# Adding the masked scores of two directions on VectorE before one product with the values

## The chip, the cores and the metric

The kernel runs on one core of a Trainium2 chip. Its engines are TensorE (PE in the profile; its weight loads are PEld), VectorE (DVE), ScalarE (ACT), GpSimd (POOL) and SyncE (SP), which here only issues transfers. The metric is the device time of one execution in microseconds; the median of three runs is given.

## The reference

Two layers of a token-mixing backbone over 512 latent tokens and 256 context tokens. The change lies in the gated linear attention of the token mixer, which runs forward (f) and backward (b) over chunks of 64 tokens and adds the two results:

```
g_mid  = g[:, :, GLA_CHUNK // 2 - 1][:, :, None]
scores = jnp.einsum('bnihd,bnjhd->bnhij', q * jnp.exp(g - g_mid), k * jnp.exp(g_mid - g))
scores = jnp.where(mask, scores, 0.0)
o_intra = jnp.einsum('bnhij,bnjhv->bnihv', scores, v)
o_inter = jnp.einsum('bnihd,nbhdv->bnihv', q * jnp.exp(g), s_start)
...
o = o_f + flip(o_b)
o = o * lax.rsqrt(jnp.mean(o * o, axis=-1, keepdims=True) + RMS_EPS)
```

There are 4 heads with keys of 64 and values of 128 elements. `v` is the same in both directions, so `scores_f @ v + scores_b @ v` equals `(scores_f + scores_b) @ v`. The mask keeps s <= t forward and s >= t backward within a chunk.

## The kernel before

Activations lie feature-major, [128 partitions, tiles, tokens]. Each weight matrix streams in from memory in chunks (`stream`), and is split for precision: ACT rounds a chunk to `w_hi` (L1202), POOL computes the rest `w_lo` = `raw` - `w_hi` (L840), and PE multiplies three times per tile (`split_matmul`, L903). Nearly all of PE's work is these products.

The order of all work is one list, `ORDER`, built by hand in `build_order`; every engine walks it and does its own part of each entry. The attention output of a layer is done tile by tile, a tile being 128 tokens: six tiles in layer 0 (context and latent), four in layer 1. After the first two `gate` entries and the position transform (`dft`), the loop over tiles appends for tile number a:

```
order.append(("score", L, tt))
if a == 0: order.append(("halves", L))
if a + 1 < len(tiles): ... ("gate", L, tiles[a + 1], g)   # g = 0 and 1
if a: order.append(("msq", L, tiles[a - 1]))
order.append(("o", L, tt))
if a == 0: order.append(("fold", L))
```

What the engines do for these entries:

- `gate` of a tile and direction: PE sums the decays over tokens (L1044), ACT takes three exponentials of it into `E` (L1375 to L1377), DVE multiplies them with q, k and q (L1767, L1768, L1769), and says so by `qk_ready`.
- `score`: PE multiplies decayed k and q of both directions and four heads into the PSUM tile `N` (L1057, 16 instructions in the trace). DVE copies them under the mask from `N` to `Pm` (L1777, four instructions), a tile in SBUF that was set to zero once per layer (L1764).
- `o`: PE multiplies values (`vtok`, the stationary side) with `Pm` (L1069: 4 heads by 2 directions, each two instructions in the trace, so 16 a tile, in two groups of 8), and the chunk states `S` with `E` (L1075, 32 in the trace), all summed in PSUM tile `A`. ACT squares the result into `osq` (L1384).
- `msq`: PE takes means of the squares (L1083), ACT Ln and Exp (L1395, L1396), DVE scales by it and by the gate `r` (L1786, L1791 four times), ACT rounds (`h_hi`, L1398), DVE takes the rest (`h_lo`, L1795).
- `halves` and `fold`, once per layer: the halves of the position transform are copied (L1745) and folded (L1754, L1758) on DVE, rounded on ACT (L1364), and POOL takes the rest (L868).

After `o` of the second and third tile ACT also rounds two weight chunks (`high`, L1202), which POOL follows with L840. After the last `msq` comes `wout`, whose products (L903) wait for the last `h_lo`. `Pm` and `E` have two buffers, by the tile's turn `b`.

Of the kernel before, what the change touches and what calls it, by code (L numbers as in the profile page):

```python
# [14 lines left out]
P = 128  # L15
# [4 lines left out]
HEADS, DK, DV, RANK, CHUNK = 4, 64, 128, 16, 64  # L20
# [418 lines left out]
def bass_hybrid_block(nc: bass.Bass, stream, pairs, modw, xT, pos_row, pos_col, cols, wdec, masks, mats, wide, x_keep, out):  # L439
    with ExitStack() as ctx:  # L440
        def sb(name, shape, dt=F32, stack=None):
            return (stack or ctx).enter_context(nc.sbuf_tensor(name, shape, dt))

        def sem(name):
            return ctx.enter_context(nc.semaphore(name))
# [73 lines left out]
        with mix:  # L519
            kT = sb("kT", [P, 2, TOK], stack=mix)  # L520
            qT = sb("qT", [P, 2, TOK], stack=mix)
            ktok = sb("ktok", [P, TT_ALL, KW], stack=mix)
            vtok = sb("vtok", [P, TT_ALL, VW], stack=mix)
            ls = sb("ls", [P, TT_ALL, 2 * KW], stack=mix)
            S = sb("S", [P, 2, 12, 2, DV], stack=mix)
            r_s = sb("r_s", [P, 4, TOK], stack=mix)
            early, late = ExitStack(), ExitStack()
            with early:
                lrT = sb("lrT", [33, TOK], stack=early)
                eu = sb("eu", [P, 2, KW], stack=early)  # L530
                vst = sb("vst", [P, 2, TOK], stack=early)
                zs = sb("zs", [P, 2, 2 * KW], stack=early)
                cgz = sb("cgz", [P, 2, TOK], stack=early)
                bg = sb("bg", [P, 2, TOK], stack=early)
            uF = vst
            fy = ktok[:, :, :].rearrange("p (c a) b -> p c (a b)", c=2)
            cv = zs[:, :, :].rearrange("p a b -> p (a b)")[:, 0:TOK]
            with late:
                E = sb("E", [P, 2, 2, 3, 2, P], stack=late)

                Pm = sb("Pm", [P, 2, 2, 2, 2, P], stack=late)
                osq = sb("osq", [P, 4 * P], stack=late)
                rb = sb("rb", [P, 2, 4, P], stack=late)

# [29 lines left out]
            sem("ssq_ready"), sem("rstd_ready"), sem("xnew_ready"), sem("sq_ready"), sem("sq_used"))  # L574
        haff_ready, hhi_ready = sem("haff_ready"), sem("hhi_ready")
        yn_ready = sem("yn_ready")
        hlo_ready_p, hlo_ready_v = sem("hlo_ready_p"), sem("hlo_ready_v")
        pair_in, sums_ready, f_hi, f_lo, f_used = (
            [sem(f"pair_in{j}") for j in range(2)], sem("sums_ready"), sem("f_hi"), sem("f_lo"), sem("f_used"))
# [13 lines left out]
        def nth(L, tt):  # L593

            return 6 * L + tiles_of(L).index(tt)
# [5 lines left out]
        def read_out(eng, e):  # L601

            for u, before in PLAN.before[e]:
                eng.wait_ge(free[u], before + 1)
# [57 lines left out]
        def o_at(b, h):  # L662
            pr, hp = divmod(h, 2)
            return A[b][:, hp * 512 + pr * P:hp * 512 + (pr + 1) * P]
# [226 lines left out]
        def _(pe):  # L891
# [23 lines left out]
            for e in ORDER:  # L915
                kind, L = e[0], e[1]
                n0 = PLAN.n0[e]
                if kind == "modk":
                    g, k = e[2:]
# [5 lines left out]
                    for j in range(4):  # L925
                        mm = pe.matmul(dst[32 * j:32 * j + 32, 0:512], csil[:, k, :], piece_at(p)[:, 512 * j:512 * j + 512],  # L926
                                       start=(k == 0), stop=(k == KT - 1))
# [15 lines left out]
                elif kind == "head":  # L943
# [13 lines left out]
                    m = project(dst, n, [parts(("nrm",) + pre)[s]], H, ready=lambda k: h_wait(pe, *pre, s, k))  # L957
# [7 lines left out]
                elif kind == "z":  # L965
                    tt = e[2]
# [5 lines left out]
                              start=True, stop=True).then_inc(full["z"], 1)  # L972
                elif kind == "turn":
# [4 lines left out]
                    for tt in range(TT_ALL):  # L978
                        m = pe.transpose(G[tt // 4][:, (tt % 4) * P:(tt % 4 + 1) * P], src[:, tt * P:(tt + 1) * P], ident[:, :])
                    m.then_inc(full["turn"], 1)  # L980
                elif kind == "suffix":
                    g, tt = STEPS[e[2]]
                    unit_free(e)
                    if PLAN.full[e] == 1:
# [3 lines left out]
                              start=True, stop=True)  # L988
                    for pr in range(2):
                        m = pe.matmul(N[:, 768 + 2 * pr:770 + 2 * pr], ls[:, tt, g * KW + pr * P:g * KW + (pr + 1) * P],  # L990
                                      mat[:, 768:770], start=True, stop=True)
                    m.then_inc(full["suffix"], 1)
                elif kind == "dstate":
                    g, tt = STEPS[e[2]]
# [4 lines left out]
                    for c in range(2):  # L999
                        for pr in range(2):  # L1000
                            for hp in range(2):
                                h, row = 2 * pr + hp, slice(c * 64, c * 64 + 64)
                                m = pe.matmul(G[c][hp * 64:hp * 64 + 64, pr * DV:(pr + 1) * DV],  # L1003
                                              eu[row, g, h * DK:(h + 1) * DK], vtok[row, tt, h * DV:(h + 1) * DV],
                                              start=True, stop=True)
                    m.then_inc(full["dstate"], 1)
                elif kind == "four":
                    tt = e[2]
# [3 lines left out]
                    for ch in range(2):  # L1012
                        m = pe.matmul(unit_of(e)[:, ch * 256:(ch + 1) * 256], uF[:, ch, tt * P:(tt + 1) * P], chan[:, :],
                                      start=True, stop=True)
                    m.then_inc(full["four"], 1)
                elif kind == "dft":
# [10 lines left out]
                    for ch in range(2):  # L1027
                        for a, tt in enumerate(tts):
                            for part in range(2):
# [6 lines left out]
                                for p, (l, r) in enumerate(((lhs[0], w_hi), (lhs[0], w_lo), (lhs[1], w_hi))):  # L1036
                                    m = pe.matmul(dst, l, r[:, s, o:o + w], start=(first and p == 0), stop=(last and p == 2))  # L1037
                    m.then_inc(chunk_used, 1)
                elif kind == "gate":
                    tt, g = e[2], e[3]  # L1040
# [6 lines left out]
                elif kind == "score":  # L1047
                    tt = e[2]
                    b = turn(L, tt)
# [9 lines left out]
                elif kind == "o":  # L1059
# [2 lines left out]
                    unit_free(e)  # L1062
                    read_out(pe, ("score", L, tt))
                    read_out(pe, ("dstate", L, 11))
                    for pr in range(2):
                        for g in range(2):
                            for hp in range(2):
                                h = 2 * pr + hp
                                pe.matmul(o_at(b, h), vtok[:, tt, h * DV:(h + 1) * DV], Pm[:, b, hp, g, pr, :],  # L1069
                                          start=(g == 0), stop=False)  # L1070
                        for g in range(2):
                            for c in range(2):
                                for hp in range(2):
                                    row = slice(hp * 64, hp * 64 + 64)
                                    m = pe.matmul(o_at(b, 2 * pr + hp)[:, c * 64:c * 64 + 64], S[row, g, 2 * tt + c, pr, :],  # L1075
                                                  E[row, b, g, 2, pr, c * 64:c * 64 + 64], start=False,
                                                  stop=(g == 1 and c == 1))
# [443 lines left out]
        def _(dve):  # L1521
            steps = [0]

            def link(ins):

                steps[0] += 1
                ins.then_inc(dve_step, 1)
                dve.wait_ge(dve_step, steps[0])
# [124 lines left out]
            for e in ORDER:  # L1653
# [106 lines left out]
                elif kind == "gate":  # L1760
                    tt, g = e[2], e[3]
                    b = turn(L, tt)
                    if tiles_of(L).index(tt) == 0 and g == 0:
                        link(dve.memset(Pm[:, :, :, :, :, :], 0.0))  # L1764
                    read_out(dve, e)
                    q_, k_ = qT[:, :, tt * P:(tt + 1) * P], kT[:, :, tt * P:(tt + 1) * P]
                    dve.tensor_tensor(E[:, b, g, 0, :, :], E[:, b, g, 0, :, :], q_, ALU.mult)  # L1767
# [2 lines left out]
                elif kind == "score":  # L1770
# [3 lines left out]
                        dve.wait_ge(full["o"], nth(L, e[2]) - 1)  # L1774
                    for hp in range(2):
                        for g in range(2):
                            m = dve.copy_predicated(Pm[:, b, hp, g, :, :],  # L1777
                                                    mask[:, g:g + 1, :].to_broadcast([P, 2, P]),
                                                    N[:, hp * 512 + g * 256:hp * 512 + (g + 1) * 256].rearrange("p (r t) -> p r t", r=2))
                        m.then_inc(free[f"N{hp}"], 1)  # L1780
                elif kind == "msq":
                    tt = e[2]
                    b, q = turn(L, tt), nth(L, tt)
# [283 lines left out]
```

## Time and profile before

| | |
|---|---|
| median of 3 runs | 1699.17 us (1696.13 to 1702.62) |
| the profiled execution | 1701.38 us |
| its span in the trace | 1699.6 us |
| PE busy | 1604.2 us (94%) |
| DVE / ACT / POOL busy | 733.6 / 568.3 / 615.0 us |
| mean granted clock of TensorE | 0.974 of full speed |
| tile loop of layer 0 | 301.70 to 359.06 us |
| tile loop of layer 1 | 1196.00 to 1235.90 us |

The execution time is the span and 1.8 us around it. The two stretches of the last rows are 97 of the 1699.6 us; only they hold the instructions that the change touches, but for one memset shortly ahead of each.

### The profile page before, as it was taken

How to read it: one execution, taken by the hardware profiler on the slowest of the kernel's cores; microseconds unless marked ns; L12 is line 12 of the kernel's file. 1: busy time of each engine (PE TensorE's matmuls, PEld its weight loads, DVE VectorE, ACT ScalarE, POOL GpSimd, SP SyncE). 2: the span in 40 equal slices, each digit the busy share in tenths (PEclk: the TensorE clock that was granted, in tenths of full speed). 3: DMA queues.
4: the chain of work that ended last, by engine and by line, in shares of the span. 5: the costliest groups of instructions: out<-in, count | busy, mean ns of one | idle time of the engine just before them, and what ended most of it. 6: DMA issues, size and time to landing. Idle time of an engine off the chain costs nothing.

```text
span 1699.6 us, 22343 instructions
## 1 busy us (share of the span) xinstructions
PE 1604.2 (94%) x8868; PEld 1328.9 (78%) x8868; DVE 733.6 (43%) x1109; ACT 568.3 (33%) x897; POOL 615.0 (36%) x317
## 2 busy tenths in 40 slices
PE   5899999999899999999999989999997999999995
PEld 2678877877589989998999757887872888888884
DVE  2510225745555614662366764045735221221235
ACT  3624212423643412441143354432513322222221
POOL 1512211314333623563255433232232444444442
PEclk9899999999999999999999999999998999999997
DMA  9334332135512212212222672121161322332321
GB/s 373 149 124 149 124 131 75 63 112 169 203 63 75 75 50 75 75 62 66 72 75 103 219 284 64 63 75 50 39 260 62 99 91 95 99 98 87 99 78 59
DMA packets 48220, 186.21 MB, mean 110 GB/s; under 512 B 5062, under 2 KB 8006, under 8 KB 40968
## 3 DMA queue, kind: packets, MB, share of 16 engines
q1 hardware_dynamic: 44028, 170.29, 29.4%
q10 hardware_dynamic: 4108, 14.75, 2.3%
q8 instruction: 59, 0.97, 0.2%
q14 instruction: 25, 0.20, 0.0%
HBM read 173.49 MB, written 11.53 MB: 109 GB/s over the span
## 4 chain that ended last, share of the span: by engine, by line
PE 85%; DVE 6%; ACT 4%; DMA 2%; issue 1%; SPq 1%; POOL 0%; DVEq 0%; ACTq 0%; POOLq 0%
PE A L903 59%; PE A L1135 7%; PE N L1135 4%; PE G L1135 4%; PE G L1179 1%; PE G L926 1%; DMA raw<-modw 1%; PE N L926 1%; PE A L1037 1%; PE G L1003 1%; PE N L987 1%; DVE E L1768 1%; DVE rb L1791 1%; DVE y L1928 1%; ACT w_hi L1202 1%
## 5 line engine op out<-in xcount | busy, mean ns | idle before, releaser
L840 POOL TENSOR_TENSOR w_lo<-raw,w_hi 128x1024 fp32r<-128x1024 f32 (+2 forms) x183 | 422.2, 2310 | 752.8 <-ACT w_hi L1202 752.8
L903 PE MATMUL A<-h_hi,w_hi 128*128 128x512 f32 (+1 forms) x1232 | 420.4, 373 | 26.2 <-DVE h_lo L1935 16.0
L903 PE MATMUL A<-h_hi,w_lo 128*128 128x512 f32 (+1 forms) x1232 | 412.1, 366 | 0.0
L903 PE MATMUL A<-h_lo,w_hi 128*128 128x512 f32 (+1 forms) x1232 | 411.9, 366 | 0.0
L1202 ACT ACTIVATE w_hi<-raw 128x1024 fp32r<-128x1024 f32 (+2 forms) x183 | 184.6, 1012 | 479.7 <-PE A L903 416.4
L903 PEld LDWEIGHTS A<-h_hi,w_hi 128*128 128x128 f32 x1232 | 219.9, 192 | 86.0 <-issue 27.4
L903 PEld LDWEIGHTS A<-h_hi,w_lo 128*128 128x128 f32 x1232 | 220.5, 193 | 37.6
L903 PEld LDWEIGHTS A<-h_lo,w_hi 128*128 128x128 f32 x1232 | 220.2, 193 | 35.9 <-issue 0.2
L903 PE MATMUL A<-g_hi,w_hi 128*128 128x512 f32 (+1 forms) x528 | 169.4, 360 | 2.1 <-DVE g_lo L1650 2.0
L903 PE MATMUL A<-g_lo,w_hi 128*128 128x512 f32 (+1 forms) x528 | 168.4, 358 | 0.0
L903 PE MATMUL A<-g_hi,w_lo 128*128 128x512 f32 (+1 forms) x528 | 168.4, 358 | 0.0
L880 POOL TENSOR_TENSOR w_lo<-w_sum,w_hi 128x512 fp32r<-128x512 f32 x45 | 81.4, 1834 | 144.6 <-DVE w_sum L1577 98.8
L1708 DVE TENSOR_TENSOR eu<-eu,ktok 128x256 f32<-128x256 f32 x24 | 35.5, 1479 | 188.4 <-ACT dec L1342 188.3
L903 PEld LDWEIGHTS A<-g_hi,w_hi 128*128 128x128 f32 x528 | 90.8, 188 | 23.5 <-issue 4.4
L903 PEld LDWEIGHTS A<-g_lo,w_hi 128*128 128x128 f32 x528 | 90.5, 188 | 16.5 <-issue 0.2
L903 PEld LDWEIGHTS A<-g_hi,w_lo 128*128 128x128 f32 x528 | 90.7, 188 | 16.3
L1229 ACT ACTIVATE w_hi<-w_sum 128x512 fp32r<-128x512 f32 x81 | 49.2, 625 | 119.8 <-DVE w_sum L1577 119.7
L1896 DVE TENSOR_TENSOR sqb<-sqb,A 128x512 f32<-128x512 f32 x22 | 15.1, 687 | 157.2 <-PE A L903 157.2
L1899 DVE TENSOR_TENSOR g_lo<-sqb,g_hi 128x512 f32 x22 | 50.5, 2295 | 23.2 <-ACT g_hi L1452 23.2
L885 POOL TENSOR_TENSOR h_lo<-y,h_hi 128x512 fp32r<-128x512 f32 (+1 forms) x28 | 31.6, 1133 | 75.2 <-ACT h_hi L1499 74.9
L1820 DVE COPY y<-A 128x512 f32<-128x512 f32 (+1 forms) x24 | 16.6, 692 | 90.3 <-PE A L903 90.3
L880 POOL TENSOR_TENSOR w_lo<-raw,w_hi 128x512 fp32r<-128x512 f32 x27 | 39.0, 1460 | 31.5 <-ACT w_hi L1229 31.5
(256 smaller groups left out, 2332.4 us busy)
## 6 DMA issues: line engine op xcount, KB each, us to landing
raw<-stream SPq DMA_DIRECT2D x150, 512.0 KB, 3.6
mraw<-modw SPq DMA_DIRECT2D x38, 1024.0 KB, 5.3
x<-x_keep ACTq DMA_DIRECT2D x6, 1536.0 KB, 9.3
raw<-pairs SPq DMA_DIRECT2D x18, 512.0 KB, 4.7
raw<-stream SPq DMA_DIRECT2D x24, 384.0 KB, 3.1
raw<-modw SPq DMA_DIRECT2D x6, 1024.0 KB, 14.7
mraw<-pairs SPq DMA_DIRECT2D x9, 512.0 KB, 3.7
x_keep<-x SPq DMA_DIRECT2D x4, 768.0 KB, 22.3
```

What stands on the lines that cost most here:

```text
L840: pool.tensor_tensor(w_lo[:, n % RING, 0:WIDTH[n]], raw[:, n % RAW, 0:WIDTH[n]], w_hi[:, n % RING, 0:WIDTH[n]].bitcast(F32), ALU.subtract) ...
L880: pool.tensor_tensor(lo, src, f_weight(w_hi, q, pos).bitcast(F32), ALU.subtract).then_inc(f_lo, 1)
L885: pool.tensor_tensor(h_lo[:, k, t0:t1], y[:, k, t0:t1], h_hi[:, k, t0:t1].bitcast(F32), ALU.subtract).then_inc(hlo_ready_p, 1)
L903: m = pe.matmul(dst[:, t0:t1], a, b[:, k, t0:t1], start=(first and p == 0), stop=(last and p == 2))
L926: mm = pe.matmul(dst[32 * j:32 * j + 32, 0:512], csil[:, k, :], piece_at(p)[:, 512 * j:512 * j + 512], start=(k == 0), stop=(k == KT - 1))
L987: pe.matmul(N[:, 512:512 + KW], mat[:, 512 + g * P:512 + (g + 1) * P], ls[:, tt, g * KW:(g + 1) * KW], start=True, stop=True)
L1003: m = pe.matmul(G[c][hp * 64:hp * 64 + 64, pr * DV:(pr + 1) * DV], eu[row, g, h * DK:(h + 1) * DK], vtok[row, tt, h * DV:(h + 1) * DV], st ...
L1135: m = pe.matmul(dst, a[:, cols], b[:, k, :], start=(k == 0 and p == 0), stop=(k == 3 and p == 2))
L1202: act.activation(w_hi[:, n % RING, 0:width], src, ACT.Copy).then_inc(hi_done, 1)
L1229: act.activation(f_weight(w_hi, q, pos), src, ACT.Copy).then_inc(f_hi, 1)
L1708: dve.tensor_tensor(eu[:, g, :], eu[:, g, :], ktok[:, tt, :], ALU.mult).then_inc(ku_ready, 1)
L1899: dve.tensor_tensor(g_lo[:, gp, 0:T], sqb[:, 0:1, 0:T], g_hi[:, gp, 0:T].bitcast(F32), ALU.subtract).then_inc(g_ready, 1)
```

## The change

The masked scores of the two directions are no longer both multiplied with the values. After the four masked copies of a tile DVE adds the two halves of `Pm` to a new tile `Ps`, and says so by a new semaphore `p_ready`. PE waits for it ahead of `o`, and multiplies values with `Ps` once per head: in the trace 8 instructions a tile instead of 16. `Pm` is now single-buffered (half as large, as is the memset), and `Ps` has the two buffers.

```
-                Pm = sb("Pm", [P, 2, 2, 2, 2, P], stack=late)
+                Pm = sb("Pm", [P, 2, 2, 2, P], stack=late)
+                Ps = sb("Ps", [P, 2, 2, 2, P], stack=late)
...
+                    pe.wait_ge(p_ready, nth(L, tt) + 1)
                     for pr in range(2):
-                        for g in range(2):
-                            for hp in range(2):
-                                h = 2 * pr + hp
-                                pe.matmul(o_at(b, h), vtok[:, tt, h * DV:(h + 1) * DV], Pm[:, b, hp, g, pr, :],
-                                          start=(g == 0), stop=False)
+                        for hp in range(2):
+                            h = 2 * pr + hp
+                            pe.matmul(o_at(b, h), vtok[:, tt, h * DV:(h + 1) * DV], Ps[:, b, hp, pr, :],
+                                      start=True, stop=False)
...
-                        link(dve.memset(Pm[:, :, :, :, :, :], 0.0))
+                        link(dve.memset(Pm[:, :, :, :, :], 0.0))
...
-                            m = dve.copy_predicated(Pm[:, b, hp, g, :, :],
+                            m = dve.copy_predicated(Pm[:, hp, g, :, :],
...
                         m.then_inc(free[f"N{hp}"], 1)
+                    read_out(dve, e)
+                    dve.tensor_tensor(Ps[:, b, :, :, :], Pm[:, :, 0, :, :], Pm[:, :, 1, :, :], ALU.add).then_inc(p_ready, 1)
```

On DVE, in the middle of layer 0 (the second tile's `score`, then the `gate` of the third and the `msq` of the first), the program's order was this, with the semaphores that a row waits for in brackets:

```order
L1777 COPY_PREDICATED Pm<-mask,N 128x256 [waits full_score]
L1777 COPY_PREDICATED Pm<-mask,N 128x256 x3
L1767 TENSOR_TENSOR E<-E,qT 128x256 [waits free_G0]
L1768 TENSOR_TENSOR E<-E,kT 128x256
L1769 TENSOR_TENSOR E<-E,qT 128x256
L1767 TENSOR_TENSOR E<-E,qT 128x256 [waits free_G1]
L1768 TENSOR_TENSOR E<-E,kT 128x256
L1769 TENSOR_TENSOR E<-E,qT 128x256
L1786 TENSOR_TENSOR rb<-A0,rb 128x512 [waits orstd_ready]
```

and is now this (the lines have moved by two and more):

```order
L1779 COPY_PREDICATED Pm<-mask,N 128x256 [waits full_score]
L1779 COPY_PREDICATED Pm<-mask,N 128x256 x3
L1784 TENSOR_TENSOR Ps<-Pm 128x512 [waits free_N1,free_N0]
L1769 TENSOR_TENSOR E<-E,qT 128x256 [waits free_G0]
L1770 TENSOR_TENSOR E<-E,kT 128x256
L1771 TENSOR_TENSOR E<-E,qT 128x256
L1769 TENSOR_TENSOR E<-E,qT 128x256 [waits free_G1]
L1770 TENSOR_TENSOR E<-E,kT 128x256
L1771 TENSOR_TENSOR E<-E,qT 128x256
L1790 TENSOR_TENSOR rb<-A0,rb 128x512 [waits orstd_ready]
```

One instruction has come in, between the masked copies and the six multiplications of the next tile; it waits for the copies' own semaphores.

On PE, from the first tile's gate products to the second tile's scores, stood:

```order
L1044 MATMUL G<-mat,ls 128x256 [waits free_G1]
L1044 MATMUL G<-mat,ls 128x256
L1069 MATMUL A<-Pm,vtok 128x128 [waits free_G0,free_N1,free_G1,free_N0,free_A0]
L1069 MATMUL A<-Pm,vtok 128x128 x3
L1075 MATMUL A<-E,S 128x64 x8
L1069 MATMUL A<-Pm,vtok 128x128 x4
L1075 MATMUL A<-E,S 128x64 x8
L1057 MATMUL N<-E 128x128 [waits qk_ready,free_N1,free_N0]
```

and stands now:

```order
L1046 MATMUL G<-mat,ls 128x256 [waits free_G1]
L1046 MATMUL G<-mat,ls 128x256
L1071 MATMUL A<-Ps,vtok 128x128 [waits free_G0,free_G1,free_N1,p_ready,free_N0,free_A0]
L1071 MATMUL A<-Ps,vtok 128x128
L1077 MATMUL A<-E,S 128x64 x8
L1071 MATMUL A<-Ps,vtok 128x128 x2
L1077 MATMUL A<-E,S 128x64 x8
L1059 MATMUL N<-E 128x128 [waits qk_ready,free_N1,free_N0]
```

Half of the value products are gone, and the first of the rest waits for `p_ready` as well. (An f32 product of the program is two instructions in the trace: the 4 a tile that are left will be 8 there.) ACT, POOL and SP have the same order as before.

## Rows read from the trace of the kernel before

**Rows 1.** The page: busy times, and the chain that ended last by engine.
```profile
PE 1604.2 (94%) x8868; PEld 1328.9 (78%) x8868; DVE 733.6 (43%) x1109; ACT 568.3 (33%) x897; POOL 615.0 (36%) x317
...
PE 85%; DVE 6%; ACT 4%; DMA 2%; issue 1%; SPq 1%; POOL 0%; DVEq 0%; ACTq 0%; POOLq 0%
```

**Rows 2.** Windows, the two tile loops: length, busy PE, PEld, DVE, ACT, POOL, clock, DMA.
```profile
301.70:359.06 57.36, 49.66 (x461) 42.65 (x461) 43.86 (x102) 29.25 (x64) 13.51 (x6) 1.00 0.12 38
1196.00:1235.90 39.90, 34.69 (x309) 29.91 (x308) 28.75 (x64) 20.28 (x42) 12.05 (x6) 0.96 0.14 41
```

**Rows 3.** Groups by line: busy us, mean ns of one, idle before.
```profile
L1069 PE MATMUL A<-Pm,vtok 128*128 128x128 f32 x160 | 23.4, 291 | 2.1 <-issue 1.2 <-ACT E L1377 0.6
...
L1764 DVE MEMSET Pm<- 128x2048 f32 x2 | 3.5, 1765 | 0.8 <-issue 0.8
```

**Rows 4.** Chain that ended last, layer 0, third tile: start, us, what.
```profile
321.37 0.93 DVE E L1767
322.30 2.50 DVE E L1768
324.79 0.33 DVE E L1769
...
326.13 0.61 DVE rb L1786
```

**Rows 5.** Timeline of DVE, the same tile: start, us, instruction, idle before.
```profile
318.17 0.69 DVE L1795 TENSOR_TENSOR h_lo<-rb,h_hi 128x512 fp32r<-128x512 f32 x1 [0.69 <-ACT h_hi L1398]
318.78 1.44 DVE L1777 COPY_PREDICATED Pm<-mask,N 128x256 f32<-128x256 int32 x4
321.37 0.93 DVE L1767 TENSOR_TENSOR E<-E,qT 128x256 f32<-128x256 f32 x1 [1.15 <-ACT E L1377]
```

**Rows 6.** Timeline of POOL, layer 0, second and third tile.
```profile
310.29 3.79 POOL L868 TENSOR_TENSOR h_lo<-ktok,h_hi 128x768 fp32r<-128x768 f32 x2 [13.30 <-ACT h_hi L1364]
319.65 4.86 POOL L840 TENSOR_TENSOR w_lo<-raw,w_hi 128x1024 fp32r<-128x1024 f32 x2 [5.57 <-ACT w_hi L1202]
```

**Rows 7.** Timeline of PE, the third tile.
```profile
320.44 1.13 PE L1069 MATMUL A<-Pm,vtok 128*128 128x128 f32 x8
321.50 1.11 PE L1075 MATMUL A<-E,S 64*128 64x64 f32 x16
...
326.28 1.16 PE L1057 MATMUL N<-E 64*128 64x128 f32 x16 [1.55 <-DVE E L1769]
```

**Rows 8.** Timeline of DVE, layer 0, first tile and the fold's end.
```profile
302.89 1.44 DVE L1777 COPY_PREDICATED Pm<-mask,N 128x256 f32<-128x256 int32 x4 [3.54 <-PE N L1057]
304.23 1.14 DVE L1745 COPY ktok<-A 128x257 f32<-128x257 f32 x4
...
309.14 0.62 DVE L1758 SCALAR_TENSOR_TENSOR ktok<-ktok 128x255 f32<-128x255 f32 x2
```

**Rows 9.** Timelines of DVE, PE and ACT, the last tile of layer 0.
```profile
346.56 1.43 DVE L1777 COPY_PREDICATED Pm<-mask,N 128x256 f32<-128x256 int32 x4 [0.35 <-PE N L1057]
348.20 1.13 PE L1069 MATMUL A<-Pm,vtok 128*128 128x128 f32 x8 [0.63 <-issue]
352.55 0.60 ACT L1384 ACTIVATE osq<-A 128x512 f32<-128x512 f32 x1 [1.02 <-PE A L1075]
```

**Rows 10.** Timeline of layer 1: the second tile's copies, then the last tile.
```profile
1204.15 1.44 DVE L1777 COPY_PREDICATED Pm<-mask,N 128x256 f32<-128x256 int32 x4 [1.24 <-PE N L1057]
...
1222.38 1.44 DVE L1777 COPY_PREDICATED Pm<-mask,N 128x256 f32<-128x256 int32 x4
1223.25 4.67 POOL L840 TENSOR_TENSOR w_lo<-raw,w_hi 128x1024 fp32r<-128x1024 f32 x2 [5.57 <-ACT w_hi L1202]
...
1226.12 2.74 DVE L1791 SCALAR_TENSOR_TENSOR rb<-rb,par,r_s 128x128 f32<-128x128 f32 x4
```

**Rows 11.** Timeline of PE, the last tile of layer 1.
```profile
1224.03 2.05 PE L1069 MATMUL A<-Pm,vtok 128*128 128x128 f32 x8
```

**Rows 12.** Windows around it, columns as in rows 2.
```profile
1220.00:1225.00 5.00, 3.20 (x20) 2.24 (x17) 3.12 (x9) 3.85 (x6) 1.75 (x1) 0.78 0.12 46
```

More of the change, by code:

```diff
@@ L576, in bass_hybrid_block @@
         yn_ready = sem("yn_ready")
+        p_ready = sem("p_ready")
         hlo_ready_p, hlo_ready_v = sem("hlo_ready_p"), sem("hlo_ready_v")
```

## The prediction

> **What bounds the kernel now.** I read the page first: PE is busy for 94% of the span and has 85% of the chain that ended last [rows 1]. That speaks for a change that takes work from PE, but it is an average over stages. So I read the windows of the two tile loops next, the only places where scores meet values. There PE is busy for 49.66 of 57.36 us in layer 0 and 34.69 of 39.90 us in layer 1 [rows 2]. It is idle for 13% of both, so something else sets the pace for at least part of them. The chain tells what: in the third tile it runs over DVE's six multiplications of E (321.37 to 326.13) and on into DVE's msq [rows 4]. PE waits for them: its next scores start at 326.28 after 1.55 us of idling for L1769 [rows 7].
>
> The second thing to see is why those six take 4.76 us. One takes 0.33 us alone (L1769), but the first took 0.93 and the second 2.50 [rows 4]. POOL ran two subtractions over SBUF from 319.65 to 324.51 [rows 6]. L1767 ended at 322.30, just past their middle (319.65 + 2.43 = 322.08), and L1768 at 324.79, just past their end. So a DVE instruction with two SBUF operands stands still while a POOL subtraction runs; one gets in between two of them. The masked copies, which read N from PSUM, took their 1.44 us though POOL began in their midst [rows 5, 6]. DVE and POOL thus form one serial chain here: DVE's idle time before L1767, 1.15 us in the rows [rows 5], would have gone to waiting for POOL anyway, since POOL's first subtraction ran until 322.08.
>
> **The change, part by part.**
>
> Removed on PE: a group of 8 products takes 1.06 us (320.44 to 321.50) [rows 7]. There are two groups a tile, each halved: 1.06 us a tile, 10.6 us over ten tiles, 80 of 160 instructions [rows 3]. It is a gain only where the end of o is what comes last.
>
> Added on DVE: one addition of 512 elements. The nearest row is L1795, 0.69 us, with the same size and two SBUF operands [rows 5]; its successor starts 0.61 us after it. Without a wait DVE overlaps neighbours: the four copies take 1.44 us, but the next instruction started 1.34 us after their start [rows 8]. The new wait on the copies' semaphores forbids that, 0.14 us more (0.10 of overlap and an estimated 0.04 of start). So a tile costs 0.61 to 0.75 us of DVE; I take 0.75. The products can start when the addition is done, 1.44 + 0.03 + 0.69 = 2.16 us after the copies' start, not 1.44: 0.72 us later.
>
> The rule on same-engine order speaks to that wait: the Trainium skill (VectorE: DVE Perf Modes, The DRAIN you can't avoid) says that a semaphore between two VectorE instructions costs nothing extra. By it a tile would cost 0.61, and the sum below be some 0.8 us less. The overlap of 0.10 us in the rows speaks against it.
>
> The addition reads two operands in SBUF, so I expect it to be held like L1768, and to hold POOL in turn. That is the place where a rule speaks against the change: the Trainium skill (SBUF — State Buffer, SBUF: two separate sides) says that of a VectorE instruction with two SBUF inputs and a GpSimd one the first to start has the shared ports for its whole length, and the other blocks fully. By that rule the addition takes the gap between POOL's two subtractions and L1767 must wait for the second. Without the rule it would lie in DVE's 1.15 us of idle time and cost nothing in such tiles.
>
> Now tile by tile, as delay of DVE against before. **Layer 0.** Tile 1: DVE runs on without a pause from halves to the fold's end at 309.76 (309.14 + 0.62) [rows 8], and from there into the copies of tile 2, so +0.75. Tile 2: the addition waits for the first L868 of POOL. L868 starts 0.1 or 0.2 us after before at most, since ACT rounds the fold as soon as it is done. Worked through with 1.73 us for one L868 (3.79 less the gap, halved) the delay grows to +0.85 at the msq. But the fold, which ended at 309.76, will end at 310.5, and POOL starts about 310.25 (310.29 before) [rows 6, 8]; if POOL gets in first, that fold instruction and the second L868 are each late, and the delay is +1.95. Tiles 3 and 4: POOL's pair of L840, then the six; +0.75 each. Tile 5: no POOL, DVE without a pause; +0.75. Before the copies of the last tile DVE idled 0.35 us for PE [rows 9]; that is taken up: -0.35. Last tile: products start 0.72 us later after the copies and are 1.06 us shorter: -0.34. The rest (osq at 352.55 and after it) only shifts. Sum: 0.85 + 3 x 0.75 - 0.35 - 0.34 = +2.4 us, or +3.5 with the fold collision.
>
> **Layer 1.** Tile 1: DVE waited 1.24 us for PE's scores before the second tile's copies [rows 10], and PE gets there 0.34 us sooner; the 0.75 us is hidden. Tile 2: POOL's two L868 and the six end about where they did: 0. Tile 3: POOL's L840 pair: +0.75. Tile 4, the last: the copies start at 1222.38 + 0.75, POOL at 1223.25 + 0.75 [rows 10], each subtraction 2.33 us. The addition waits until 1226.3 and ends at 1227.0. Only then does the second subtraction start, and it holds the four L1791 until 1229.3; they end at 1230.45. Before they began at 1226.12 and ended at 1228.86: +1.6. So +1.6 us, with the products at full clock.
>
> What they may not be: in this very tile the granted clock was 0.78 over 5 us, of which PE was busy for 3.20 [rows 12], and the 8 products at its start took 2.05 us instead of 1.13 [rows 11, 7]. A mean of 0.78 between the two levels of 2.4 and 1.2 GHz is 2 x 0.22 x 5 = 2.2 us at the lower one, which costs PE 1.1 us. PE will idle longer here, since the addition holds it off until 1227.2; with as long a stretch at 1.2 GHz inside o, o ends up to 1.1 us after L1791's chain needs it: +1.6 to +2.7.
>
> The smaller memset (1.76 us before [rows 3], half the elements now) lies under the position transform's products on PE, which PE works through before the first scores. It gives nothing, and its absence would cost nothing.
>
> **Sum.** Between 2.4 + 1.6 = +4.0 and 3.5 + 2.7 = +6.2 us; both open terms are near even, so I take the middle, +5.1. (At 0.61 us a tile instead of 0.75 the lower end is +3.2.) Against the profiled execution (1701.38) that is 1706.5; it ran 2.2 us above the median of the runs, 1699.17, so the forecast is **1704.2 us**, 0.3% more. A difference under 0.5% (8.5 us) can't be told from none here; my forecast is in that band.
>
> **The rivals.**
>
> - PE sets the pace, the additions hide. For it: the 94% [rows 1]. Against: 1.55 us of waiting for DVE in one tile [rows 7]. It would give all 10.6 us: 1688.6, faster. Chance 0.04.
> - PE's o sets the pace, but the addition lies in front of it: -1.06 + 0.72 = -0.34 a tile, ten tiles, 1695.8. For it: at the end of layer 0 ACT waits for o [rows 9]. Or the addition falls in DVE's idle time everywhere: within 2 us of 1699. Together 0.14, no difference.
> - The clock. PE does less and idles up to 3 us before o in tiles 3 and 4 of layer 0 (the addition waits for POOL). An episode as above costs 1.1 us of PE's path. In tiles 3 and 4 a slow o still ends before DVE is through; it decides only if the fall reaches tiles 5 and 6 of layer 0 and the first products after each loop. It takes four such episodes on the path besides my sum, 1699.2 + 5.1 + 4.4 = 1708.7, slower. Against: gaps of 1.55 us there left the clock at 1.00 [rows 2, 7]. Chance 0.10.
> - The rest, 0.72, is my forecast, with its own range 1701 to 1707.
>
> **How the numbers follow.** Faster by over 0.5% needs the first rival: 0.04. Slower by over 0.5% (over 1707.7) needs the clock: 0.10. The same: 0.86. The range goes from the forecast's side down to 1698, which takes in the second rival's milder form and the spread of a median (the runs lie 6.5 us apart), and up to 1709, the clock's case.
>
> **What would show it.** PE: L1069's successor with 80 instructions, busy time in the two loops about 10 us less, idle before it about 2 to 3 us in tiles 3 and 4. DVE: ten additions of 0.69 us, but about 2.4 us for those of layer 0 tiles 3 and 4 and layer 1 tiles 3 and 4; then L1767, not L1768, is the one that takes about 2.5 us. The loops' lengths 57.4 and 39.9 us become about 60.3 and 42. POOL's pairs grow from 4.86 to about 5.2 us. I am wrong if the additions take 0.69 us beside POOL, if the six E instructions don't end later, or if the loops get shorter. Outside the loops nothing should move.

## The result: 0.3% slower, and the profile after

| | before | changed |
|---|---|---|
| median of 10 runs | 1698.72 us (1694.10 to 1702.62) | 1702.11 us (1699.74 to 1706.74) |
| ratio | 1 | 1.0029 (1.0016 to 1.0042) |
| profiled execution / span | 1701.38 / 1699.6 us | 1706.06 / 1704.2 us |
| mean granted clock of that execution | 0.974 | 0.968 |
| loop of layer 0 | 56.11 us | 60.12 us |
| loop of layer 1 | 38.65 us | 43.70 us |
| between the loops | 838.2 us | 834.1 us |
| behind the second | 463.7 us | 462.0 us |

A second measurement of the changed kernel gave 1.0028 (1.0014 to 1.0042), and the kernel before measured against itself 1.0003 (0.9988 to 1.0018). (In that second measurement one slow run of each kernel, 2287 and 4046 us, is left out of the ratio.) So the slowdown is real. By the ratio it is 4.9 us (2.7 to 7.1); the medians of the table are 3.4 us apart, those of the second measurement 4.2. The forecast was 1704.2 us, +5.1.

A loop is counted here from its first masked copy to the end of its last h_lo. The two windows of the changed kernel over these stretches (length, busy PE, PEld, DVE, ACT, POOL, granted clock, DMA) answer to [rows 2], and below them stand the same two stretches of the kernel before:

```profile
304.26:364.38 60.12, 49.88 (x396) 41.45 (x396) 49.77 (x108) 28.32 (x60) 14.39 (x6) 0.89 0.12 36
1198.48:1242.18 43.70, 35.48 (x260) 28.91 (x260) 34.06 (x68) 19.83 (x40) 12.73 (x6) 0.80 0.12 37
...
302.89:359.00 56.11, 48.48 (x444) 41.57 (x444) 43.85 (x102) 28.25 (x60) 13.51 (x6) 1.00 0.12 39
1197.21:1235.86 38.65, 33.48 (x292) 28.82 (x292) 28.75 (x64) 19.62 (x40) 12.05 (x6) 0.96 0.14 42
```

PE executes 80 instructions fewer (48 and 32), and yet is busy 1.4 and 2.0 us longer: the clock column has gone from 1.00 and 0.96 to 0.89 and 0.80. The loops together are 9.1 us longer, not 5. Between and behind them the profiled execution is 5.8 us shorter, and its first loop began 1.4 us later.

The groups by line, in place of [rows 3]: 80 products instead of 160, and ten additions that take on average twice what one takes alone (1.42 against 0.69 us).

```profile
L1071 PE MATMUL A<-Ps,vtok 128*128 128x128 f32 x80 | 16.0, 329 | 11.5 <-DVE Ps L1784 11.5
...
L1784 DVE TENSOR_TENSOR Ps<-Pm 128x512 f32<-128x512 f32 x10 | 14.2, 1423 | 1.0
```

The timeline of DVE in the third tile answers to [rows 5]:

```profile
320.31 0.69 DVE L1799 TENSOR_TENSOR h_lo<-rb,h_hi 128x512 fp32r<-128x512 f32 x1 [0.70 <-ACT h_hi L1400]
320.92 1.43 DVE L1779 COPY_PREDICATED Pm<-mask,N 128x256 f32<-128x256 int32 x4
322.46 2.23 DVE L1784 TENSOR_TENSOR Ps<-Pm 128x512 f32<-128x512 f32 x1
324.61 2.57 DVE L1769 TENSOR_TENSOR E<-E,qT 128x256 f32<-128x256 f32 x1
327.10 0.41 DVE L1770 TENSOR_TENSOR E<-E,kT 128x256 f32<-128x256 f32 x1
```

and that of POOL to [rows 6]:

```profile
311.72 4.16 POOL L870 TENSOR_TENSOR h_lo<-ktok,h_hi 128x768 fp32r<-128x768 f32 x2 [13.37 <-ACT h_hi L1366]
321.79 5.11 POOL L842 TENSOR_TENSOR w_lo<-raw,w_hi 128x1024 fp32r<-128x1024 f32 x2 [5.91 <-ACT w_hi L1204]
```

The addition starts at 322.46 inside POOL's first subtraction and ends at 324.69, 0.55 us past the end of that one (324.14). The multiplication of E with q, first of the six, then waits for the second subtraction; before the change it was the multiplication with k, second of the six, that did [rows 4]. POOL's pair has grown from 4.86 to 5.11 us, since POOL is held too: its second subtraction takes 2.80 us, 2.55 before. This is the place that the prediction named.

PE's timeline, in place of [rows 7 and 9], tiles 3 and 5 of layer 0, and the last tile's copies on DVE:

```profile
324.83 0.68 PE L1071 MATMUL A<-Ps,vtok 128*128 128x128 f32 x4 [2.89 <-DVE Ps L1784]
325.45 1.22 PE L1077 MATMUL A<-E,S 64*128 64x64 f32 x16
326.59 1.22 PE L1071 MATMUL A<-Ps,vtok 128*128 128x128 f32 x4
...
345.33 0.68 PE L1071 MATMUL A<-Ps,vtok 128*128 128x128 f32 x4 [1.34 <-DVE Ps L1784]
345.95 1.24 PE L1077 MATMUL A<-E,S 64*128 64x64 f32 x16
347.11 1.22 PE L1071 MATMUL A<-Ps,vtok 128*128 128x128 f32 x4
348.26 1.97 PE L1077 MATMUL A<-E,S 64*128 64x64 f32 x16
350.02 2.02 PE L1059 MATMUL N<-E 64*128 64x128 f32 x16
...
352.10 1.44 DVE L1779 COPY_PREDICATED Pm<-mask,N 128x256 f32<-128x256 int32 x4 [1.73 <-PE N L1059]
```

After 2.89 and after 1.34 us of waiting PE starts at full clock, and falls to 1.2 GHz within its work (the clock records of the trace have the lower level from 326.3 and from 346.8, each time for 6.8 us): the second group of four products takes 1.22 us, not 0.71. In tile 5 that matters, since the next scores come out late and DVE, which had waited 0.35 us for them before, waits 1.73. The chain of the last tile of layer 1 shows the dearest place:

```profile
1226.21 2.24 DVE Ps L1784
1228.45 0.14 issue
1228.59 1.19 PE A L1071 x4
1229.78 1.90 PE A L1077 x16
1231.69 1.15 PE A L1071 x4
1232.84 1.93 PE A L1077 x16
1234.76 0.02 issue
1234.79 0.60 ACT osq L1386
```

Addition, then o at half clock all through (6.2 us), then the squares at 1234.79. The window says the same, granted clock 0.50 over ten microseconds:

```profile
1225.00:1235.00 10.00, 7.80 (x44) 6.17 (x43) 7.14 (x11) 3.57 (x6) 5.11 (x2) 0.50 0.15 52
```

This fall doesn't begin with the wait for the sum. The clock records have it from 1224.0, 2.2 us ahead of the addition and 25.5 us after the loop's first copies. The kernel before falls at the same place, 25.6 us after its first copies (1222.8), but for 3.4 us only; here the lower level lasts 17.1 us.

### The profile page after: what moved, and what is told of

Read it like the earlier page. It is cut to its first block, busy times and chain, and to the rows that moved or that the text cites. A ratio compares the mean times of both kernels' runs of the same rounds, so it can differ in the third digit from the quotient of the medians.

```text
span 1704.2 us, 22213 instructions
## 1 busy us (share of the span) xinstructions
PE 1602.5 (94%) x8788; PEld 1324.7 (78%) x8788; DVE 741.9 (44%) x1119; ACT 568.2 (33%) x897; POOL 615.5 (36%) x317
## 4 chain that ended last, share of the span: by engine, by line
PE 84%; DVE 8%; ACT 3%; DMA 2%; issue 1%; SPq 1%; POOL 0%; DVEq 0%; ACTq 0%; POOLq 0%
PE A L905 58%; PE A L1137 7%; PE N L1137 4%; PE G L1137 4%; PE G L1181 1%; PE G L928 1%; DMA raw<-modw 1%; PE N L928 1%; DVE Pm L1779 1%; DVE Ps L1784 1%; PE A L1039 1%; PE G L1005 1%; PE N L989 1%; DVE E L1769 1%; DVE x L1922 1%
```

## The experiments

Each was profiled and timed in five rounds against the kernel before. All that follows is measured from a loop's first masked copies. The columns of layer 0 are the copies of the third and fifth tile (before: 15.89 and 36.74 us; changed: 16.66 and 38.70) and the loop's length.

| kernel | tile 3 | tile 5 | layer 0 | layer 1 | clock in both | ratio |
|---|---|---|---|---|---|---|
| before, again | 15.88 | 36.73 | 56.11 | 38.65 | 1.00, 0.96 | 1.0003 |
| changed, again | 16.65 | 38.71 | 59.17 | 43.69 | 0.91, 0.80 | 1.0028 |
| addition alone | 16.66 | 38.72 | 58.91 | 43.31 | 0.97, 0.80 | 1.0042 |
| addition and wait | 17.22 | 39.27 | 60.10 | 46.46 | 0.94, 0.82 | 1.0074 |
| products alone | 15.36 | 36.23 | 54.28 | 38.70 | 0.94, 0.87 | 0.9969 |
| addition twice | 19.41 | 44.65 | 69.25 | 50.51 | 0.80, 0.73 | 1.0147 |
| idle products | 16.64 | 38.69 | 60.36 | 40.14 | 0.94, 1.00 | 1.0017 |
| GpSimd quiet | 16.65 | 31.29 | 60.33 | 44.54 | 0.92, 0.86 | 1.0074 |
| merged masks | 15.37 | 36.23 | 54.99 | 39.53 | 0.94, 0.83 | 0.9973 |
| merged, early weights | 21.61 | 35.40 | 53.84 | 37.83 | 0.94, 0.86 | 0.9954 |

My theory was that of the prediction: DVE with POOL sets the pace and the addition lengthens it. The rivals were TensorE's late start, and its clock.

**The addition alone** (add_only), with TensorE as before:

```
+ read_out(dve, e)
+ dve.tensor_tensor(mrow[:, :].rearrange("p (h r t) -> p h r t", h=2, r=2), Pm[:, b, :, 0, :, :], Pm[:, b, :, 1, :, :], ALU.add).then_inc(p_ready, 1)
```

> The kernel before plus the ten additions on VectorE, whose result nobody reads (it goes to an idle tile); TensorE keeps its 16 products a tile and doesn't wait. If VectorE's time beside GpSimd sets the pace, the addition alone costs most of what the change cost: the two loops, from the first masked copies to the first product of wout (56.2 and 38.7 us before, 60.2 and 43.8 with the change), become some 59 and 40.5 us, and the additions beside a GpSimd subtraction take 2.2 us. If instead the later start of o or TensorE's clock costs the time, the loops stay within 1 us of 56.2 and 38.7 us and the ratio to the kernel before is 1.000.

Ratio 1.0042 (1.0027 to 1.0056), layer 0 58.9 us, layer 1 43.3. DVE's delays are those of the changed kernel to 0.02 us in tiles 3 and 5, though nobody waits for the sum. So the addition alone is enough for a slowdown of this size; TensorE's wait for it isn't needed (what the wait adds to it is measured below). Layer 1 came out above the expected 40.5 us: its granted clock was 0.80 here too, at the lower level for 17.1 us as in the changed kernel. TensorE waits longer for what DVE delays (1.90 us instead of 0.71 ahead of the last scores of layer 1), and its clock falls without a late sum.

**Half the products alone** (fewer_products):

```
- for g in range(2):
-     for hp in range(2):
-         h = 2 * pr + hp
-         pe.matmul(o_at(b, h), vtok[:, tt, h * DV:(h + 1) * DV], Pm[:, b, hp, g, pr, :], start=(g == 0), stop=False)
+ for hp in range(2):
+     h = 2 * pr + hp
+     pe.matmul(o_at(b, h), vtok[:, tt, h * DV:(h + 1) * DV], Pm[:, b, hp, 0, pr, :], start=True, stop=False)
```

> The kernel before with 8 products a tile in place of 16 and nothing added: the backward scores are left out of the output. If TensorE isn't what the loops wait for, halving its products is worth about 1 us in each layer's last tile, loops of about 55 and 38 us, ratio 0.999. If TensorE set the pace, it would be worth 10.6 us, ratio 0.994. If longer idling lowers the granted clock, the loops get no shorter at all, with a window below 1.00 that was at 1.00 before.

Ratio 0.9969 (0.9955 to 0.9982). The steps from tile 3 to tile 5 are untouched (20.87 us, 20.85 before), so TensorE doesn't set the pace there; the gain in the loop is 0.5 us in the first two tiles and 1.3 in the rest. In layer 1 the loop got no shorter (38.70 against 38.65 us): its granted clock fell from 0.96 to 0.87, as the last of the three expectations says. But 5.3 us by the ratio (3.1 to 7.6) is more than the 1.8 us of the loops, and I had expected about 2. The rest lies behind the loop of layer 1: that stretch takes 459.1 us here and 463.7 in both profiles of the kernel before. By the clock records TensorE is at 1.2 GHz for 29.1 us of it instead of 39.9, and half of that difference is 5.4 us. The time for wout's first 180 chained products, 41.12 us against 42.68 in the control, is 1.6 us of it. This is one profile, the fastest of the twelve runs (1687.1 us), so it shows where time was saved and not that all 5.3 us lie there. Why the clock falls less there isn't shown.

**The addition, the wait, and all 16 products** (add_wait): the edit of add_only, and

```
+ pe.wait_ge(p_ready, nth(L, tt) + 1)
```

> The kernel before plus the additions and TensorE's wait for them, but still 16 products a tile from the unsummed tile; the changed kernel is this with 8 products fewer. By the step table VectorE's delays are those of the addition alone (third tile's copies at 16.66 us after the first). If fewer products gain 1.06 us only in the last tile, the loops take about 1 us more than the changed kernel's at the same granted clock, so 58 to 61 us in layer 0; if the late start of o is what counts, they lie clearly above those of the addition alone (58.9 and 43.3 us).

Ratio 1.0074 (1.0055 to 1.0093). The wait adds 0.0032 to the addition alone, and halving the products takes 0.0046 off again, 7.8 us. So the two halves of the change are worth about +12.5 us (addition and wait) and -7.8 us (products in the kernel with the wait). The latter are worth 5.3 us in the kernel before; by their intervals the two can't be told apart. The step table didn't hold: the third tile's copies came at 17.22 us, not 16.66. The expectation that fewer products gain only 1 us was wrong in layer 1, 46.46 against 43.70 us: the last copies come 1.05 us later, and the last o is 1.71 us longer (7.91 against 6.20), with 8 products more at half clock. In layer 0 the loops are 60.10 here and 60.12 and 59.17 in the changed kernel.

**The addition twice** (two_adds):

```
+ link(dve.tensor_tensor(Ps[:, b, :, :, :], Pm[:, :, 0, :, :], Pm[:, :, 1, :, :], ALU.add))
```

> The changed kernel with the addition made twice, the second behind a wait on the first. If VectorE and GpSimd are one serial chain in the loops, the second costs 0.6 to 0.8 us a tile again: copies of the fifth tile at about 41.5 us after the first tile's (38.7 changed, 36.7 before), ratio to the kernel before about 1.005 to 1.007. If the addition only fills a gap that is there anyway, the second is free in the tiles beside GpSimd and the fifth tile's copies stay below 40 us.

Ratio 1.0147 (1.0127 to 1.0167), far above 1.005 to 1.007. DVE's timeline in tiles 4 and 5 shows why:

```profile
334.78 2.23 DVE L1784 TENSOR_TENSOR Ps<-Pm 128x512 f32<-128x512 f32 x1
337.05 2.72 DVE L1785 TENSOR_TENSOR Ps<-Pm 128x512 f32<-128x512 f32 x1
339.69 0.41 DVE L1769 TENSOR_TENSOR E<-E,qT 128x256 f32<-128x256 f32 x1
...
347.92 1.44 DVE L1779 COPY_PREDICATED Pm<-mask,N 128x256 f32<-128x256 int32 x4 [2.98 <-PE N L1059]
```

DVE's own step is as expected: the second addition takes the second wait for POOL, the E multiplications then run freely, and the serial chain is about 0.7 us longer (tile 4 to tile 5 takes 14.67 us, 11.69 without the wait for scores, 11.02 in the changed kernel). But the sum is ready only when both are through, o starts that late at a falling clock, and DVE waits 2.98 us for scores. Once o comes last, a delay costs more than its own length.

**Idle products in the waits** (filler), with 6 calls of the same kind ahead of the last squares of layer 1:

```
+ if 2 <= tiles_of(L).index(tt) < 5:
+     for _ in range(5):
+         pe.matmul(o_at(b, 0), one_v[:, :], ident[:, :], start=True, stop=True)
```

> The changed kernel with idle products of constants put in where TensorE waits for the sums in tiles 3 to 5 of layer 0 and 3 and 4 of layer 1 (10 instructions each, 1.4 us), and 12 more where it waits for the squares ahead of the last tile of layer 1. Their results are overwritten. If the clock's falls inside the loops cost what lies above the worked sum, the granted clock stays at 1.00 there and the loops shrink from 60.2 to about 58.3 and from 43.8 to about 40.5 us, though TensorE has more to do; part of it is lost again when wout starts at the lower clock. If the clock doesn't matter, the loops stay at 60 and 44 us or get longer.

In layer 1 the granted clock stayed at 1.00 and the loop fell from 43.70 to 40.14 us, as the clock theory said (40.5). In layer 0 it didn't help: the copies of the last tile came at 46.02 us instead of 47.84, which they also do in the second profile of the changed kernel without idle products, and the clock then fell at the end, so that the loop took 60.36 us. Ratio 1.0017 (1.0003 to 1.0031), against 1.0029 of the changed kernel: the intervals overlap, so only the loop of layer 1 is shown. The runs do show that the clock isn't the whole loss: the mean granted clock of the twelve is 0.978, that of the kernel before in the same rounds 0.976, and they are still slower.

**GpSimd quiet** (quiet):

```
- if 1 <= tiles_of(L).index(e[2]) < 3:
-     for j in range(2):
-         high(PLAN.n0[("wout", L)] + 2 * tiles_of(L).index(e[2]) - 2 + j)
+ if e[2] == tiles_of(L)[-1]:
+     for j in range(4):
+         high(PLAN.n0[("wout", L)] + j)
```

> The changed kernel with the four roundings of wout's weights moved on ScalarE from the second and third tile to behind the last, so that GpSimd does nothing in tiles 3 and 4. If it is GpSimd's subtractions that hold the addition, it takes 0.69 us in those tiles, and a tile's step falls from 11.0 us to about 7.5 to 8.5; the loops lose 5 to 6 us in layer 0, of which some comes back, since wout's weights are ready later. If the additions still take 2.2 us there, GpSimd has nothing to do with it.

```profile
322.95 0.69 DVE L1784 TENSOR_TENSOR Ps<-Pm 128x512 f32<-128x512 f32 x1
323.57 0.42 DVE L1769 TENSOR_TENSOR E<-E,qT 128x256 f32<-128x256 f32 x1
...
356.69 1.06 ACT L1204 ACTIVATE w_hi<-raw 128x1024 fp32r<-128x1024 f32 x1 [5.00 <-DMA raw<-stream]
361.62 0.69 DVE L1790 TENSOR_TENSOR rb<-A,rb 128x512 f32<-128x512 f32 x1 [12.54 <-ACT rb L1398]
```

With POOL's pair out of tiles 3 and 4 the addition takes 0.69 us, and a tile's step is 7.32 us instead of 11.02. That settles it: POOL's subtractions hold the addition and the multiplication behind it, and each pair costs 3.7 us, 1.54 at the addition (2.23 against 0.69) and 2.15 at the multiplication (2.57 against 0.42). (The Trainium skill, SBUF — State Buffer, SBUF: two separate sides, states this exclusive lock; the trace agrees, 2.23 us beside POOL, 0.69 without.) The whole got slower, 1.0074 (1.0058 to 1.0090), as the last tile's rb waited 12.54 us for ACT. Two of the moved roundings, which now stand ahead of that tile's rb in ACT's order, waited 5.00 and 1.55 us for their weights to arrive (`DMA raw<-stream`): a cost that I had put too low.

**Merged masks** (merge), the same function without an addition:

```
+ dve.tensor_tensor(Ps[:, b, hp, :, :], half, mask[:, 0:1, :].bitcast(F32).to_broadcast([P, 2, P]), ALU.mult).then_inc(s_step, 1)
...
+ dve.wait_ge(s_step, steps_s[0] - 1 + hp)
+ dve.copy_predicated(Ps[:, b, hp, :, :], mask[:, 1:2, :].to_broadcast([P, 2, P]), half).then_inc(free[f"N{hp}"], 1)
...
+ fwd = (before * 1.0 + eye).astype(np.float32).view(np.int32)
+ masks = np.ascontiguousarray(np.stack([fwd, (after & ~eye.astype(bool)).astype(np.int32)], 1))
```

> The changed kernel without the addition: forward scores are multiplied on VectorE with a mask of 1, and 2 on the diagonal, straight from PSUM into the tile, and the backward scores copied over the rest under a strict mask, as on the diagonal both directions have the same score. Four VectorE instructions of 256 elements a tile as before the change, none with two operands in SBUF, and 8 products. If the addition is the whole cost, the loops fall to about 55 and 38 us, ratio to the kernel before 0.998 to 1.000. If the wait on its own semaphore between the masked writes, or fewer products and a falling clock, cost most, they stay at 58 and 41 us or more.

Ratio 0.9973 (0.9961 to 0.9985): faster than both. No masked instruction, each of which reads N from PSUM, is held by POOL. In the second tile all four run inside POOL's first subtraction, in the time that they take alone (0.76 and 0.77 us in the first tile), while a multiplication with two operands in SBUF is held:

```profile
311.22 3.69 POOL L870 TENSOR_TENSOR h_lo<-ktok,h_hi 128x768 fp32r<-128x768 f32 x2 [12.56 <-ACT h_hi L1365]
311.37 0.75 DVE L1778 TENSOR_TENSOR Ps<-N,mask 128x256 f32<-128x256 f32 x2
312.04 0.77 DVE L1784 COPY_PREDICATED Ps<-mask,N 128x256 f32<-128x256 int32 x2
313.19 2.01 DVE L1766 TENSOR_TENSOR E<-E,qT 128x256 f32<-128x256 f32 x1 [0.38 <-ACT E L1378]
...
322.54 0.92 DVE L1766 TENSOR_TENSOR E<-E,qT 128x256 f32<-128x256 f32 x1 [1.15 <-ACT E L1378]
323.38 2.57 DVE L1767 TENSOR_TENSOR E<-E,kT 128x256 f32<-128x256 f32 x1
```

In the third tile it is again the second of the six multiplications of E that is held, as in [rows 4], and the steps from tile 3 to 5 are 10.42 and 10.44 us as before the change (10.43 and 10.42). The loops are 5.1 and 4.2 us shorter than the changed kernel's. Against the kernel before they give almost nothing, -1.1 us in layer 0 and +0.9 in layer 1, where 39.53 us is above the expected 38 and the granted clock 0.83. In this profile too time is saved behind the second loop, as with half the products alone: 459.1 us instead of 463.7, of which 29.4 at 1.2 GHz.

**Merged masks, and wout's first weights rounded ahead of the loop** (merge_early): ACT's roundings leave `o` and follow the chunks of `dft`, and POOL takes four chunks more before the fold.

```
- if chunk_kind(n0 + RING) == "dft":
+ if e[2] < (3 if L else 4):
      high(n0 + RING)
...
+ high(n0 + RING)
...
- low_until(PLAN.n0[("wout", e[1])])
+ low_until(PLAN.n0[("wout", e[1])] + 4)
```

> The version without the addition (forward scores multiplied with a mask of 1 and 2, backward scores copied over the rest), and with the four roundings of wout's first weights moved on ScalarE from the second and third tile to the position transform ahead of the loop, with GpSimd's subtractions behind them. If GpSimd's subtractions cost VectorE 3.1 us in each of two tiles, as the step of 7.3 us without them against 10.4 says, the loops lose 3 to 6 us in layer 0 and 1.5 to 3 in layer 1, and the ratio to the kernel before is 0.992 to 0.996. If the subtractions now meet the fold on VectorE and the first exponentials on ScalarE instead, nothing is gained over 0.9973.

Ratio 0.9954 (0.9938 to 0.9970), loops 53.84 and 37.83 us. Steps are 6.9 us from tile 3 on, but the first copies-to-copies step has grown from 6.94 to 12.46 us. There the exponentials for the second tile stand on ACT behind a moved rounding that waited for its weights until 309.53 (1.34 us for the DMA), and the first multiplication of E, which waited 4.16 us for them, then takes 1.85 us beside a moved subtraction. In layer 0 less was gained than the 3 to 6 us expected, 1.2 against merge; in layer 1 it was 1.7, within the 1.5 to 3. The intervals of merge and of this one overlap a little.

**The controls** (before_again, after_again):

> The kernel before, unchanged, as a control. Its ratio should be 1.000 with an interval of about 0.0013 to either side, its loops 56.1 and 38.7 us again. The stretch between the two loops took 838.2 us in the first profile and 830 to 834 us in each of the five kernels profiled since, none of which changes it. If that is chance of the granted clock, this profile gives another value than 838, below 835; if it belongs to the kernel before, it gives 838 again.

> The changed kernel, unchanged, to see which of its parts repeat. VectorE's step table must repeat to 0.05 us up to the fifth tile (copies at 7.62, 16.66, 27.68 and 38.70 us). If the falls of the granted clock inside the loops belong to the change, they come again, with loops above 58.5 and 42 us, and the ratio to the kernel before is 1.002 to 1.004; if they were chance of one profile, the loops lie near the worked sums, 58.0 and 41.5 us.

The loops of the kernel before came out the same to 0.01 us. The changed kernel repeated DVE's steps up to tile 5, and layer 1 to 0.01 us, so the long fall of the clock there belongs to the change. In layer 0 it didn't all repeat: o of tile 5 ran at full clock this time after the same wait,

```profile
345.29 0.68 PE L1071 MATMUL A<-Ps,vtok 128*128 128x128 f32 x4 [1.35 <-DVE Ps L1784]
345.90 1.11 PE L1077 MATMUL A<-E,S 64*128 64x64 f32 x16
346.94 0.71 PE L1071 MATMUL A<-Ps,vtok 128*128 128x128 f32 x4
```

and the last tile's copies came at 46.02 us after the first, not 47.84. The stretch between the loops took 834.35 and 832.04 us in these profiles of the kernels before and changed, 838.2 and 834.1 in the first ones, and 830.1 to 834.8 in the other kernels; of these only quiet and merge_early move work near it, the roundings at its two ends, and they took 834.8 and 832.9. So single profiles differ by as much as the whole effect outside the loops, and 838.2 was the highest of all. The stretch behind the second loop repeats better: 463.7 us twice before, 462.0 and 461.3 changed.

## Why the prediction was right, point by point

The total was right in sign and size, and in size partly by luck. The prediction put +4.0 to +6.2 us into the loops and nothing outside; measured are +9.1 and +8.1 us in the loops, and outside 4.4 and 4.5 us less. Of its terms, those of VectorE held; the clock's was too small inside the loops, and what came back behind them was missing.

- **What sets the pace.** Right: DVE with POOL. The addition alone gives DVE's delays, the halved products leave the steps of tiles 3 to 5 as they were.
- **The addition's price.** Right in tiles beside POOL, where it takes POOL's gap: 2.23 us (said 2.4), and then a multiplication of E 2.57 (2.5). A step there grew by 0.59 us (11.02 against 10.43), not 0.75, as the wait of 0.14 us hides under POOL. Where DVE runs freely it was 0.82: in tile 1 the addition started 1.55 us after the copies (305.81 against 304.26) instead of 1.34 for an instruction without a wait, so 0.21 for the wait and 0.61 for the work. The step of that tile grew by only 0.68 us (7.62 against 6.94), as the kernel before left 0.07 us free ahead of the next copies, which now overlap with the fold. The rule that such a wait costs nothing (the Trainium skill, VectorE: DVE Perf Modes, The DRAIN you can't avoid) doesn't hold here.
- **Fold collision.** It was priced half in, and didn't happen: DVE's last fold instruction was already on its way when POOL came (311.68 against 311.72), and POOL's first subtraction took 1.93 us, 1.83 before. The rest of the growth of its pair, from 3.79 to 4.16 us, is the second subtraction, which waits for the addition as in the later tiles. Second tile: +0.09 us (said +0.10).
- **Layer 0's sum.** Said +2.4 (without the collision), measured +4.01 and +3.06. Without falls of the clock it was right: in the control the last copies came 2.36 us later than before (said 2.75), and the squares 5.82 us behind them instead of 5.99 (-0.17, said -0.34), together +2.19. On top comes 1.2 GHz, at another place each time: in o of tile 5 in the first profile (1.8 us), in the last means in the control (0.9 us). "A slow o still ends before DVE is through" held in tiles 3 and 4.
- **Layer 1's sum.** Said +1.6 to +2.7, measured +5.05 and +5.04. **This is the term that was mis-sized.** The part without the clock was right: with idle products, where the clock stays at 1.00, the loop is 1.49 us longer than before (said 1.6), and the four L1791 (now L1795) end 1.46 us later after the first copies in the changed kernel. The place was right too (last tile, addition, POOL, o). But the stretch at 1.2 GHz was priced at 1.1 us, from the 2.2 us of it that lie in the window of [rows 12]; it lasted 17.1 us, and cost 3.6: o ended 2.6 us after L1791's chain needed it (said up to 1.1), and from the squares to the end it took 0.95 us more than before. All of o ran at 0.50 (6.20 us from its start to the squares, 3.44 at full clock in the last tile of layer 0), and so did the means of the squares, L1085 (2.07 against 1.13).
- **Outside the loops.** "Nothing should move" was wrong, and so was "busy time in the two loops about 10 us less" for PE: it rose by 1.4 and 2.0 us. wout's first 180 chained products behind the loop of layer 1 took 42.74 and 42.68 us in the two profiles before, 41.13 and 41.11 in the two changed: the clock is granted in full there (1.00 against 0.83 over ten microseconds). Those 1.6 us come back each time. It isn't the long fall inside the loop that brings them: with idle products there is no fall in it, and the same products take 41.11 us. What does is open. Behind layer 0 the kernel before showed both, 0.83 and 1.00, so there it is chance. With 1.6 back, the loops' 9.1 and 8.1 us would leave 7.5 and 6.5; the ratio says 4.9 (2.7 to 7.1). The medians and the two pairs of profiles agree within their scatter, and where the last one or two microseconds are isn't settled.
- **The rivals.** PE as the bound is refuted by the steps. The clock, to which I gave 0.10 as "slower by over 0.5%", made up more than half of the loss inside the loops (1.8 and 3.6 of 9.1 us in the first profile, 0.9 and 3.6 of 8.1 in the control), but not enough to reach that bound.

## What to carry to other kernels

Before moving work from an engine that is busy for 94% of the span to one at 43%, read the stage's own chain: the "idle" engine set the pace here. An instruction with two SBUF operands on VectorE stood behind whichever GpSimd subtraction was running, so its price was that of the queue it joined, and one that reads PSUM went free. If two masked halves must become one, write both into the same tile from PSUM. A change that makes TensorE wait longer can lower its granted clock, so price the work around the new gap at both levels, and ask what comes last then.

## What the runs showed that I had not expected

- The granted clock fell after a wait of 1.34 us in one profile of the changed kernel and not after 1.35 us at the same place in the other, and not after 1.55 us in the kernel before. The place of a fall isn't given by the wait ahead of it alone.
- Halving the products was worth 5.3 us in the kernel before and 7.8 us in the one that waits for the sum, both more than the loops' own shortening explains (1.8 us in the former, 2.8 in layer 1 in the latter). In the profile of the former the rest is less time at 1.2 GHz behind the second loop (29.1 us instead of 39.9); why stays open, and so does the rest of the latter.
- A wait of a VectorE instruction on its predecessor's semaphores cost 0.12 us (one semaphore, 0.73 against 0.61 between starts) to 0.21 us (two).
